# Splitting the issue of expert weights between the queues of SyncE and ScalarE, with fifteen extra products at the end of a skipped branch

## The reference

```python
def hier_moe(h, w_group, b_group, w_expert, b_expert, w_gate, w_up, w_down):
    ...                                     # 2 of 64 experts per token, from one group of 8
    def body(e, acc):
        hid = jax.nn.silu(t @ w_gate[e]) * (t @ w_up[e])
        return acc + combine[:, e, None] * (hid @ w_down[e])
    out = lax.fori_loop(0, N_EXPERTS, body, jnp.zeros_like(t))
```

## Time and profile before

| | |
|---|---|
| median of 3 runs | 1500.72 us (1500.41 to 1501.61) |
| profiled execution | 1500.7 us; its span 1499.0 us, so 1.7 us lie outside the span |
| PE busy in the span | 1305.2 us (87%) |
| DVE, ACT, POOL busy | 682.6, 274.2, 131.9 us |
| moved by DMA | 513.91 MB, mean 343 GB/s |
| loads of expert weights | all on the queue of SP |

### The profile page before, as it was taken

The page is one execution under the profiler, slowest core; times in us unless marked ns, Lnnn a source line. Parts: engine busy times, 40 slices in busy tenths (PEclk is TensorE's granted clock), DMA queues, the critical chain, the costliest instruction groups (busy, mean ns, idle before and its releaser), DMA issues.

```text
span 1499.0 us, 25656 instructions
## 1 busy us (share of the span) xinstructions
PE 1305.2 (87%) x9722; PEld 806.4 (54%) x9722; DVE 682.6 (46%) x1641; ACT 274.2 (18%) x762; POOL 131.9 (9%) x201
## 2 busy tenths in 40 slices
PE   9999999766776679999999767776679999999998
PEld 4455565433443344666565433443344875899943
DVE  3874634221222123686644221222123646699976
ACT  2153211100010001363111100010001225222200
POOL 1312000000000000211000000000000133222100
PEclk9999999898898889999999988888889999999999
DMA  8978799999999999949999999999999992654400
GB/s 290 403 283 341 289 421 404 420 421 422 422 422 422 422 421 399 368 173 419 387 420 402 420 420 420 420 421 420 421 421 389 384 362 69 211 169 170 169 29 28
DMA packets 120716, 513.91 MB, mean 343 GB/s; under 512 B 12312, under 2 KB 46812, under 8 KB 69288
## 3 DMA queue, kind: packets, MB, share of 16 engines
q1 hardware_dynamic: 118720, 507.30, 84.8%
q0 software_dynamic: 1728, 5.12, 0.9%
q10 hardware_dynamic: 168, 0.09, 0.0%
HBM read 511.39 MB, written 1.08 MB: 342 GB/s over the span
## 4 chain that ended last, share of the span: by engine, by line
PE 59%; DMA 19%; SPq 15%; issue 3%; DVE 2%; ACT 1%; ACTq 0%; DVEq 0%; POOLq 0%; POOL 0%
SPq L2040 11%; DMA ring<-in_moe_w_up 11%; PE bank L1583 10%; PE bank L2868 8%; PE bank L743 8%; PE bank L1598 4%; PE bank L1569 4%; PE bank L2903 4%; DMA BC<-in_moe_w_gate 4%; DMA BC<-in_moe_w_up 3%; PE bank L1611 3%; PE bank L2493 3%; SPq L2049 2%; PE bank L469 2%; PE bank L481 2%
## 5 line engine op out<-in xcount | busy, mean ns | idle before, releaser
L1583 PE MATMUL bank<-ring,hT 128*32 128x256 f32 (+1 forms) x2848 | 288.0, 469 | 139.9 <-DMA ring<-in_moe_w_up 62.6
L1583 PEld LDWEIGHTS bank<-ring,hT 128*32 128x32 f32 (+1 forms) x2848 | 150.8, 135 | 250.1 <-issue 196.0
L1875 DVE TENSOR_SCALAR pT<-pT 128x256 f32<-128x256 f32 x34 | 10.0, 294 | 411.7 <-ACT pT L2007 411.7
L1583 PE MATMUL bank<-BC,hT 128*32 128x256 f32 (+1 forms) x1120 | 141.9, 417 | 32.0 <-DMA ring<-in_moe_w_gate 19.2
L1569 PEld LDWEIGHTS bank<-gtab,hn 128*128 128x128 f32 x1088 | 129.3, 192 | 15.4 <-issue 14.3
L1569 PE MATMUL bank<-gtab,hn 128*128 128x128 f32 x1088 | 132.5, 275 | 0.1
L1611 PE MATMUL bank<-hT,A 128*128 128x512 f32 x256 | 118.3, 605 | 0.0
L1598 PE MATMUL bank<-ring,gtab 128*32 128x512 f32 (+1 forms) x768 | 116.8, 596 | 1.5 <-DMA ring<-in_moe_w_down 1.1
L1583 PEld LDWEIGHTS bank<-BC,hT 128*32 128x32 f32 (+1 forms) x1120 | 72.7, 122 | 67.6 <-issue 47.8
L743 PE MATMUL bank<-ring,hT 128*128 128x512 f32 (+3 forms) x288 | 99.9, 506 | 0.7 <-DMA ring<-in_diff_w_in 0.4
L2007 ACT ACTIVATE pT<-bank 128x256 f32<-128x256 f32 x34 | 13.0, 383 | 465.0 <-PE bank L1583 465.0
(11 more groups left out here) (411 smaller groups left out, 1961.5 us busy)
## 6 DMA issues: line engine op xcount, KB each, us to landing
ring<-in_moe_w_gate SPq DMA_DIRECT2D x90, 1024.0 KB, 25.1
ring<-in_moe_w_up SPq DMA_DIRECT2D x88, 1024.0 KB, 25.5
ring<-in_moe_w_down SPq DMA_DIRECT2D x88, 1024.0 KB, 26.3
BC<-in_moe_w_gate SPq DMA_DIRECT2D x38, 1024.0 KB, 25.6
BC<-in_moe_w_up SPq DMA_DIRECT2D x32, 1024.0 KB, 25.0
BC<-in_moe_w_down SPq DMA_DIRECT2D x28, 1024.0 KB, 26.5
ring<-in_w_ada SPq DMA_DIRECT2D x24, 1024.0 KB, 14.0
ring<-in_w_up SPq DMA_DIRECT2D x22, 1024.0 KB, 7.1
```

What stands on the lines that cost most here:

```text
L1583: i = nc.tensor.matmul(GATE[q * cap:(q + 1) * cap, part * FF:(part + 1) * FF], xg[:, c, q * cap:(q + 1) * cap], u[:, c, :], start=(c == 0) ...
```

## The change

For b4 to b15, and for the gates of b16, SP begins only the units of the first two experts of a block. ACT begins those of the last two, at three places of its own block: behind the gates of a block the ups of the next block (`at_gates`), behind the copy of the hidden rows the downs of the next block (`at_hidden`), and behind the copy of the downs' result the gates of the block after next (`at_end`). ACT waits for no slot by itself: each place stands behind a wait for the products that free the slots. It reads the expert numbers at the start of each block. ACT's loop becomes two passes over four blocks, and b12 to b15 are written out. Separately, in layer 0 alone, fifteen `keep_warm` products are added at the end of the body of the branch that is skipped.

```diff
+BY_SYNC = QUAD.experts // 2
...
                     skip_group_check=True)
+                    keep_warm(pe, 7, P, 15 * (1 - layer))
...
+                def last_experts(m, part, numbers):
+                    w = (gate_w, up_w, down_w)[part]
+                    for q, expert in zip(range(BY_SYNC, QUAD.experts), numbers):
+                        u = base + m + part * QUAD.experts + q
+                        act.dma_start(slot(u), w[bass.ds(expert, 1), :, :].rearrange("e (p c) n -> p (e c n)", p=P)
+                                      ).then_inc(unit_full[units[u][2]].sem, 16)
...
+                    now = None if here is None else numbers_at(here)
+                    then = None if after is None else numbers_at(after)
+                    if at_gates:
+                        act.wait_ge(*after_gates(m, kind))
+                        last_experts(*at_gates, now)
                     act.wait_ge(*(after_ups if following is not None else after_gates)(m, kind))
                     nc.scalar.activation(eb[:, 0, :], GATE[:, 0:FF], ACT.Exp, scale=-1.0).then_inc(exped.sem, 1)
...
                     copy_hidden(P).then_inc(hT_ready.sem, 1)
+                    if at_hidden:
+                        last_experts(*at_hidden, now)
                     act.wait_ge(*after_down(m, kind))
                     nc.scalar.activation(yrow[:, NB:D], SIDE[1][:, :], ACT.Copy).then_inc(rows_a.sem, 1)
+                    if at_end:
+                        last_experts(*at_end, then)
...
-                first_blocks(block)
-                with act.Fori(0, QUADS - 1) as i:
-                    block(i + 4, i * 12 + 36, QUAD, QUAD, i)
+                block(0, 0, QUAD, QUAD)
+                block(1, 12, QUAD, PAIR)
+                act.wait_ge(*ordered(1))
+                block(2, 24, PAIR, PAIR, at_hidden=(36, 1), here=PAIRED)
+                block(3, 30, PAIR, QUAD, at_gates=(36, 2), at_end=(48, 0), here=PAIRED, after=PAIRED + 4)
+                with act.Fori(0, LOOPED - 1) as i:
+                    for j in range(PER):
+                        block(i * PER + (4 + j), i * 48 + (36 + 12 * j), QUAD, QUAD, i, (48 + 12 * j, 1), (48 + 12 * j, 2),
+                              (60 + 12 * j, 0), i * 16 + (PAIRED + 4 * j + 4), i * 16 + (PAIRED + 4 * j + 8))
...
                     for j in range(PER):
-                        ordered_block(36 + 12 * j, QUAD, i * 16 + (PAIRED + 4 * j), i, (1, 2))
-                        ordered_block(48 + 12 * j, QUAD, i * 16 + (PAIRED + 4 * j + 4), i, (0,))
+                        first_experts(36 + 12 * j, i * 16 + (PAIRED + 4 * j), i, (1, 2))
+                        first_experts(48 + 12 * j, i * 16 + (PAIRED + 4 * j + 4), i, (0,))
```

More of the change, by code:

```diff
@@ L2002, in copy_hidden, with numbers_at, block @@
                                                 HID[:, 0:2 * P].rearrange("p (c n) -> p c n", c=2)[:, :, 0:rows], ACT.Copy)
-                def block(b, m, kind, following, i=None):
+                def numbers_at(place):
+                    return [act.value_load(order_i[0:1, place + q:place + q + 1] if isinstance(place, int) else
+                                           order_i[0:1, bass.ds(place + q, 1)], min_val=0, max_val=E - 1)
+                            for q in range(BY_SYNC, QUAD.experts)]
+                def last_experts(m, part, numbers):
[4 more added lines that the diff above has]
+                                      ).then_inc(unit_full[units[u][2]].sem, 16)
+                def block(b, m, kind, following, i=None, at_gates=None, at_hidden=None, at_end=None, here=None, after=None):
+                    now = None if here is None else numbers_at(here)
[3 more added lines that the diff above has]
+                        last_experts(*at_gates, now)
                     act.wait_ge(*(after_ups if following is not None else after_gates)(m, kind))
@@ L2011, in block @@
                     copy_hidden(P).then_inc(hT_ready.sem, 1)
+                    if at_hidden:
+                        last_experts(*at_hidden, now)
                     act.wait_ge(*after_down(m, kind))
                     nc.scalar.activation(yrow[:, NB:D], SIDE[1][:, :], ACT.Copy).then_inc(rows_a.sem, 1)
+                    if at_end:
+                        last_experts(*at_end, then)
                 tokens(0, 2)
-                first_blocks(block)
-                with act.Fori(0, QUADS - 1) as i:
-                    block(i + 4, i * 12 + 36, QUAD, QUAD, i)
+                block(0, 0, QUAD, QUAD)
[7 more added lines that the diff above has]
+                              (60 + 12 * j, 0), i * 16 + (PAIRED + 4 * j + 4), i * 16 + (PAIRED + 4 * j + 8))
+                for b in range(4 + (LOOPED - 1) * PER, BLOCKS - 2):
+                    m, place = 12 * b - 12, PAIRED + 4 * (b - 4)
+                    block(b, m, QUAD, QUAD, None, (m + 12, 1), (m + 12, 2), (m + 24, 0), place + 4, place + 8)
+                block(BLOCKS - 2, 3 * E - 24, QUAD, QUAD)
                 act.wait_ge(*overflow(1))
@@ L2044, in load_block, with numbers_of, first_experts @@
                     for part in parts:
-                        for q in range(n):
+                        for q in range(len(numbers)):
                             load(m + part * n + q, (gate_w, up_w, down_w)[part], numbers[q], i)
-                def numbers_of(kind, place, i=None):
+                def numbers_of(kind, place, i=None, shared_out=False):
                     return [sp.value_load(order_i[0:1, bass.ds(place + q, 1)] if i is not None else
                                           order_i[0:1, place + q:place + q + 1], min_val=0, max_val=E - 1)
-                            for q in range(kind.experts)]
+                            for q in range(BY_SYNC if shared_out else kind.experts)]
                 def ordered_block(m, kind, place, i=None, parts=(0, 1, 2)):
                     load_block(m, kind, numbers_of(kind, place, i), parts, i)
+                def first_experts(m, place, i, parts):
+                    load_block(m, QUAD, numbers_of(QUAD, place, i, True), parts, i)
                 def last_halves(m, place):
```

## The result

The change makes the kernel slower: 1504.97 us in the median of 11 runs against 1500.72 us before; the ratio, estimated over all runs, is 1.0025 (95% interval 1.0017 to 1.0032). I forecast 1499.6 us and called "no difference" the likeliest. The time lies in the stated range (1488 to 1505), but only just, and the sign is wrong.

The account below looks back on a forecast made before the run. From b6 on the stream of weight bytes through full DMA engines was taken to set the time. Layer 0 at +1.4 us and layer 1 at -2.5 gave -1.1 against 1500.7, so 1499.6 us; range 1488 to 1505.

Parts of the forecast that it names:

- no difference: Whole kernel: a time within about 0.2%, 3.0 us, of the kernel before; chance 0.45.
- Fifteen products. Not run.: Skipped branch of layer 0: the pad moves layer 1's loop by 60 instructions and ends its refetching, saving 2.8 us.
- The loop's term: Layer 1's plateau: without refetching of the loop, 2.8 of the 4.3 us lost against layer 0 go; bounds 0 and 4.3.
- The 1.5 us at b7: Layer 1: b7's ups begin 31.32 us after b6's, before the first branch back, so these 1.5 us stay lost.
- The rival that the shift doesn't help: Layer 1's loop is still fetched in each pass: +1.4 us twice, 1503.5 us; chance 0.10.
- Two queues: Both plateaus: SP's queue runs 0.55 unit ahead, so each group completes 1.4 us later, a loss of 1.4 us a layer.
- The rival that ACT's queue falls behind: ACT's later half sets every group: from 3.4 us a layer slower by over 3 us, at 6.4 us 1509.6; chance 0.15.
- the rival that two queues move more bytes: The plateaus' rate rises, each per cent worth 7.1 us a layer: 1492.5 us at one per cent; chance 0.33.
- ACT's own work: ACT's added issues and number reads per block hide in its wait for the ups: 0, at most 2 us a layer.
- The waits at b16's downs: End of layer 1: the 0.62 and 0.44 us waits for DMA go, as those weights land 2.8 us earlier.
- The sum: Both layers: +1.4 us in layer 0 and -2.5 in layer 1 give -1.1 us, so 1499.6 us.

Follow-up runs that it names:

- e5: The kernel before, one queue, with fifteen products in a small skipped branch of their own in layer 1's b0: 1497.48 us, ratio 0.9976.
- e10: The kernel before with 64 products (256 instructions) at the end of the skipped branch: 1506.07 us in one run.
- e12: The change with 8 products in place of fifteen in the skipped branch: 1502.97 us, ratio 1.0009.
- e11: The kernel before, one queue, with 8 products at the end of the skipped branch, timed: 1502.11 us, ratio 1.0008.
- e1: The kernel before with the fifteen products in the skipped branch and nothing else: 1503.19 us, ratio 1.0012.
- e4: The change with 60 instructions of long fulfilled waits in layer 1's b0 in place of the fifteen products: 1507.42 us, ratio 1.0040.
- e3: The kernel before, one queue, with 60 instructions of long fulfilled waits in layer 1's b0: 1504.59 us, ratio 1.0024.
- e9: The change without the fifteen products, SyncE beginning three experts of a block and ScalarE one: 1511.01 us, ratio 1.0065.
- e2: The change without the fifteen products, so the even split of the loads alone: 1502.78 us, ratio 1.0012.
- e8: The kernel before with 45 products (180 instructions) at the end of the skipped branch: 1503.78 us in one run.

## Why the prediction was wrong, point by point

**The step that failed is "Fifteen products. Not run."** It counted what the pad moves at one place, the loop of layer 1, and gave the other place no price. The products stand inside the branch that layer 0 skips, so the first thing they move is the target of that skip. Before, PE jumped to code that it already had; 60 instructions further the code has to be fetched, while the DMA engines are busy for 1.07 of the time (whether that lengthens the stop was not tested). The term that was missing is +3.3 us in the profiled execution, and +2.7 to +6.0 in those of the other kernels with a stop of over 1 us behind the skip. The prediction even cited the rule that says so. The Trainium skill (Runtime: NRT & Kernel Launch, Instruction fetch mechanics) states that a taken branch to code outside the window forces a fetch ahead of going on. The trace agrees with it at the skip (2.45 us). I weighed it for the loop alone, and never asked it of the branch that the diff names.

**The loop's term was right in kind and too small.** Against -2.8 us stand -4.19 us at the ups of b15 (e5). The 1.5 us at b7 that I said would stay went too: in e5 b7's ups begin 874.63 - 844.82 = 29.81 us after b6's, against 31.32 before. What the refetching costs is measured, but not explained: the 17 packets are 0.28 MB, an estimate of 0.7 us at 422 GB/s, and layer 1 gains some 4 us without them. (The stops in b8 and b12 stand ten MATMULs into the gates, which are five products and not ten as the prediction has it.) The rival that the shift doesn't help falls with e5 and e10. By the store that the same section of the Trainium skill gives PE, a loop of this length would stay wherever it lies; the 17 packets that come and go with its place show that the place in the pieces counts as well as the length.

**Two queues** cost about what I worked out, or less. Forecast were 1.4 us a layer; layer 0 measured +1.37 us at the last downs of b16 in the change, and +0.81 to +2.32 in the four other kernels with the even split, so that the change hits 1.4 so closely is in part luck. In layer 1 the pairs of kernels that differ in the queues alone give -0.05 (e12 against e11) to +1.54 us (the change against e1). For both layers the medians of four pairs give 0.9 (e12 against e11) to 2.8 us (e4 against e3), where 2.8 were forecast. The place is right as well: in e9 three units to one make the lag several times as long, so it is the lead of one queue over the other. The Trainium skill's rule (DMA: Bandwidth & Descriptors, Queues, rings and completion order), turns packet by packet, fits e9, and the landings in the change: the ups of b7 in layer 0 landed at 308.84 and 313.79 from SyncE's queue and at 310.43 and 315.24 from ScalarE's, in turn. The rival that ACT's queue falls behind would have needed a lag of 3.4 us a layer; the even split stayed below that in each kernel, and only three to one goes beyond.

**The rate on the plateaus** stayed at 422 GB/s, so the rival that two queues move more bytes falls. In layer 1 the rise from 420 came with the end of the refetching: e5, with one queue, has 422 too, and e2, with two, 420.

**ACT's own work** cost nothing: ACT waits 464.7 us for the ups, 465.0 before, and the ups of b4 and b5 in layer 0 begin 0.07 us later, as does b0. **The waits at b16's downs** in layer 1, 0.62 and 0.44 us for DMA, are gone; one for ACT is left:

```profile
1155.64 1.92 PE L1599 MATMUL bank<-ring,gtab 128*32 128x512 f32 x16 [0.47 <-ACT gtab L2003]
...
1160.36 1.92 PE L1599 MATMUL bank<-ring,gtab 128*32 128x512 f32 x16
```

They are not gone for the reason that I gave, weights that land 2.8 us earlier: in e5, where those land earlier still, the two waits stay (0.62 and 0.66 us), and in e2, without the shift, they are gone, as in e3 with one queue. What decides it is not shown.

**The sum.** Forecast were +1.4, 0 and -2.5 us, -1.1 in all. The profiled execution (1503.32 us) has +1.37, +3.31 and -2.33, +2.35 at the last downs of layer 1 and +2.5 in the span. That layer 1 comes out so near to its forecast is luck: the loop gave more than I counted (-3.87 in e1), and the 1.1 us for the waits at b16's downs had the wrong reason. The median lies 1.7 us above this execution. The stop's length varies (2.45 us in the change, 4.27 to 4.50 in e1, e8 and e10), and the eleven times of the change spread over 6.2 us, those of e5 over 1.7; that the longer runs are those with longer stops is likely, but not shown by a trace.

## What to carry to other kernels

Code that is never run has a price where it lies: whatever is added inside a skipped branch moves the target of the skip as well as all that follows, so read PE's timeline at each jump that the new code moves, not only at the one that it is meant for. A loop whose instructions are fetched again in each pass shows as packets of the instruction queue on its plateau and as idle PE that waits for "issue" just behind the loop's head; a small branch between the two places cured that here for 3.8 us (0.24%). Where the stream of bytes is already full, a second queue adds no bytes, and a group that both share waits for the slower one.

## What the runs showed of the hardware that was not expected

- A jump into code that PE did not hold cost 2.45 to 4.50 us of standstill, and the granted clock fell to 0.50 (1.2 GHz) behind it, for 3.4 us in the change; the whole price was 3.3 to 6.0 us. PE went on 2.3 to 2.7 us after an instruction packet started, in each of the fifteen stops.
- Moving the loop by 256 instructions brought the refetching back in full (72 packets for 71, with a program 256 instructions longer); moving it by 32, 60, 62 or 180 ended it.
- Sixty instructions that only wait for what is long fulfilled cost 6.57 us: 5.12 us idle, and then the low clock. No fetch stands behind it.
